# Output projection and FFN norm by quarters instead of halves, and four low-part subtractions on GpSimd

## The reference

```python
def trunk_layer(x, pos, past, mem_k, mem_v, p):
    ...                                       # three kinds of attention, x = x + mixed @ w_out
    x = x + memory_attend(x, mem_k, mem_v, p['g_mem_q'], p['w_mem_q'], p['w_mem_o'])
    y, conv_new = conv_ffn(x, conv0, p['g_ffn'], p['w_ffn_up'], p['w_ffn_conv'], p['b_ffn_conv'], p['w_ffn_down'])
    x = x + y

def memory_attend(x, mem_k, mem_v, g, w_q, w_o):
    q = (rmsnorm(x, g) @ w_q)                 # 4 heads of 128
    s = einsum(q, mem_k) * MEM_SCALE          # 256 memory tokens
    return einsum(softmax(s), mem_v) @ w_o    # 512 -> 1024

def conv_ffn(x, conv_prev, g, w_up, w_conv, b_conv, w_down):
    u = rmsnorm(x, g) @ w_up                  # 1024 -> 2 * 2816
    c = causal_conv3(u, conv_prev) + b_conv
    a, b = jnp.split(c, 2, axis=-1)
    return (jax.nn.silu(a) * b) @ w_down, ext[:, T:]
```

## Time and profile before

| | |
|---|---|
| median of 3 runs (lowest, highest) | 1674.61 us (1671.82, 1675.45) |
| the profiled execution, its own time | 1671.71 us |
| its span in the profile | 1669.9 us |
| TensorE busy (share) | 1625.0 us (97%) |
| VectorE, ScalarE, GpSimd busy | 1171.4, 675.1, 471.2 us |
| memory loop from step 8, to the end of unit 1 | 784.27 to 931.2 us of the span |

### The profile page before, as it was taken

The page is one execution under the profiler, slowest core; times in us unless marked ns, Lnnn a source line. Parts: engine busy times, 40 slices in busy tenths (PEclk is TensorE's granted clock), DMA queues, the critical chain, the costliest instruction groups (busy, mean ns, idle before and its releaser), DMA issues.

```text
span 1669.9 us, 29448 instructions
## 1 busy us (share of the span) xinstructions
PE 1625.0 (97%) x11153; PEld 1500.0 (90%) x11153; DVE 1171.4 (70%) x1602; ACT 675.1 (40%) x1283; POOL 471.2 (28%) x246
## 2 busy tenths in 40 slices
PE   9999999999999999999987999999999999999998
PEld 8999889776667799998887999999999999999987
DVE  7583577896666755437588888888888867766765
ACT  7320122586566542106344555555555542011022
POOL 2683142000000214331424333332223322433332
PEclk9999999999999999999989999999999999999999
DMA  5322110320222314316412122222222236223213
GB/s 211 99 82 83 63 62 37 111 85 16 75 90 70 115 56 152 122 38 271 173 59 69 61 79 79 79 79 78 64 65 67 79 115 230 84 78 107 88 54 114
DMA packets 71236, 155.93 MB, mean 93 GB/s; under 512 B 29680, under 2 KB 32976, under 8 KB 68336
## 3 DMA queue, kind: packets, MB, share of 16 engines
q1 hardware_dynamic: 68848, 145.33, 25.5%
q10 hardware_dynamic: 2304, 9.44, 1.7%
HBM read 119.61 MB, written 32.86 MB: 91 GB/s over the span
## 4 chain that ended last, share of the span: by engine, by line
PE 89%; DVE 5%; issue 2%; ACT 2%; POOL 1%; DMA 1%; SPq 0%; DVEq 0%; ACTq 0%; POOLq 0%
PE scores L2675 21%; PE scores L3399 20%; PE bank L2675 10%; PE bank L3399 8%; PE pair L2675 7%; PE scores L2981 3%; PE bank L3041 3%; PE pair L3065 2%; PE scores L2771 2%; PE scores L2693 1%; DVE kbuf L2203 1%; PE pair L3335 1%; PE pair L2684 1%; PE scores L3004 1%; PE pair L3099 1%
## 5 line engine op out<-in xcount | busy, mean ns | idle before, releaser
L3399 PE MATMUL scores<-c,up_w 128*128 128x288 f32 x2464 | 364.4, 297 | 10.0 <-DVE c L2431 3.2
L3399 PEld LDWEIGHTS scores<-c,up_w 128*128 128x128 f32 x2464 | 343.5, 190 | 11.8 <-issue 8.7
L1142 POOL TENSOR_TENSOR w_hi<-w_raw,zero 128x1024 fp32r<-128x1024 f32 x32 | 64.0, 2001 | 578.7 <-DVE prob L2219 262.2
L2675 PE MATMUL scores<-s_hi,w_down 128*128 128x384 f32 (+2 forms) x484 | 132.8, 334 | 0.0
L1876 ACT ACTIVATE s_hi<-s_raw 128x1152 fp32r<-128x1152 f32 x22 | 24.3, 1157 | 178.5 <-DMA s_raw<-s_mid 178.5
L2675 PEld LDWEIGHTS scores<-s_hi,w_down 128*128 128x128 f32 x484 | 88.1, 188 | 0.6
L1272 POOL TENSOR_TENSOR w_down<-down_raw,zero 128x1024 fp32r<-128x1024 f32 x20 | 37.9, 1894 | 175.4 <-PE scores L2675 80.2
L1145 POOL TENSOR_TENSOR w_lo<-w_raw,w_hi 128x1024 fp32r<-128x1024 f32 x32 | 86.6, 2707 | 2.5
L2675 PE MATMUL scores<-act_hi,w_hi 128*128 128x384 f32 x240 | 81.7, 340 | 0.9 <-POOL w_lo L1145 0.9
L2602 DVE TENSOR_TENSOR xd<-scores,xd 128x384 f32<-128x384 f32 x108 | 58.8, 553 | 33.3 <-PE scores L2675 33.3
L3399 PE MATMUL bank<-xq,up_w 128*128 128x288 f32 x528 | 79.0, 299 | 2.1 <-issue 2.1
(11 more groups left out here) (464 smaller groups left out, 4267.4 us busy)
## 6 DMA issues: line engine op xcount, KB each, us to landing
w_raw<-wstream SPq DMA_DIRECT2D x42, 512.0 KB, 3.6
s_raw<-s_mid SPq DMA_DIRECT2D x11, 1152.0 KB, 5.4
up_raw<-wstream SPq DMA_DIRECT2D x22, 512.0 KB, 4.2
x<-wstream SPq DMA_DIRECT2D x22, 512.0 KB, 4.3
s_mid<-conv SPq DMA_DIRECT2D x22, 512.0 KB, 2.8
down_raw<-wstream SPq DMA_DIRECT2D x22, 512.0 KB, 4.8
x_blk<-xT ACTq DMA_DIRECT2D x8, 576.0 KB, 4.7
x_mid<-x_blk ACTq DMA_DIRECT2D x8, 576.0 KB, 3.1
```

What stands on the lines that cost most here:

```text
L1142: pool.tensor_tensor(w_hi[:, k], w_raw[:, k], zero[:].unsqueeze(2).to_broadcast([P, KB, P]), ALU.add).then_inc(w_rounded, 1)
L2675: mm = pe.matmul(out, w[:, k, at + kb], x(kb), start=first and kb == 0 and n == 0, stop=last and kb == n_kb - 1 and n == 2)
L3399: mm = pe.matmul(bank[acc][:, 0:QF], up_w[i][:, w, tile(kb)], b[:, kb], start=i in (0, 1, 3) and kb == 0 and n == 0, stop=kb == 3 and n == ...
```

## The change

The projection goes by pairs of rows: 16 chunks of 24 matmuls, each two rows times one quarter, into a pair of banks, ordered by quarter. Six of them stand in steps 9 to 14 of the memory loop, all six in banks (1, 3); behind it the pairs (4, 5), (0, 1), (2, 3) rotate. Four weight blocks are loaded, each once; the third and fourth are split on GpSimd into tiles of their own, mo_w, once the sample scores of step 8 and of step 9 are made. Residual rows 4 to 7 are loaded before the loop, rows 0 to 3 in step 8. The norm goes by quarters of 288 columns: a square takes two rows at once, add_rows folds the two halves, and each quarter has its own sums, roots, inverse and spread on TensorE. VectorE's and ScalarE's orders of the stage are written anew. The low parts of factors 5 and 6 of each half move from VectorE to GpSimd (part_low); there those of p = 0 stand behind the last weight low part of unit 0, those of p = 1 behind two weight sums of unit 1. The loads of unit 1's weights wait for low_made too. Two weight roundings on ScalarE and two low parts on GpSimd of the reloaded blocks go.

The core of the diff: the tables, the two new parts of GpSimd's queue, and the end of VectorE's step in the memory loop (TensorE's memory_output moves by one step likewise).

```diff
-MO_ROWS = ((0, 1), (2, 3), (6, 7), (4, 5))
-MO_CHUNKS = [(m, h) for pair in MO_ROWS for m in pair for h in range(2)]
-MO_EARLY = 7
-MO_BANKS = [(1, 3)[d % 2] for d in range(MO_EARLY)] + [0] + [(2, 4, 0, 3, 1, 5)[d % 6] for d in range(N_MO - 8)]
+MO_ROWS = ((6, 7), (4, 5), (0, 1), (2, 3))
+MO_CHUNKS = [(slot, q) for q in range(4) for slot in ((0, 1, 2, 3) if q < 3 else (2, 3, 0, 1))]
+MO_EARLY = 6
+MO_BANKS = [(1, 3)] * MO_EARLY + [((0, 1), (2, 3), (4, 5))[(d + 2) % 3] for d in range(N_MO - MO_EARLY)]
+SUM_BEHIND, SPREAD_BEHIND = {6: 0, 9: 1, 13: 2}, {7: 0, 10: 1, 14: 2}
...
+            for n in range(2):
+                slot = W_MO + 2 + n
+                k = slot % 2
+                pool.wait_ge(w_loaded[k], 16 * (slot // 2) + 16)
+                pool.wait_ge(ms_ready, NTILE + 1 + n)
+                pool.tensor_tensor(mo_w[n][:, 0], w_raw[:, k], zero[:].unsqueeze(2).to_broadcast([P, KB, P]),
+                                   ALU.add).then_inc(w_rounded, 1)
+                pool.wait_ge(w_rounded, slot - 1)
+                pool.tensor_tensor(mo_w[n][:, 1], w_raw[:, k], mo_w[n][:, 0].bitcast(F32),
+                                   ALU.subtract).then_inc(w_split, 1)
...
+            def part_low(i, p):
+
+                pool.wait_ge(x_rounded, part_rounded(i, p))
+                if p:
+                    pool.wait_ge(b_made, made_no("combined", p, 3))
+                pool.tensor_tensor(act_lo_of(i, p), x_source(i, p), act_hi_of(i, p).bitcast(F32),
+                                   ALU.subtract).then_inc(low_made, 1)
+
+            part_low(5, 0)
+            part_low(6, 0)
             up_sum_3(1)
             up_sum_2(1)
+            part_low(5, 1)
+            part_low(6, 1)
...
-                if 0 <= n - NTILE < MO_EARLY:
-                    memory_residual(n - NTILE)
+                if n - NTILE >= 4:
+                    add_square(0, n - NTILE - 3)
+                if n - NTILE == 6:
+                    add_rows(0)
+                if 0 < n - NTILE <= MO_EARLY:
+                    memory_residual(n - NTILE - 1)
```

More of the change, by code:

```diff
@@ L194, in part_split, with made_no, part_made, summed_no @@
 def part_split(i, p):
[L195 to L206, removed]
+    return 2 * KB + 5 * p + PART_LO[p].index(i) + 1
+B_ORDER = [step for p in range(2) for step in
+           [("scaled", 2 * p + h, half) for h in range(2) for half in range(2)] + [("combined", p, n) for n in range(4)]]
+def made_no(*which):
+    return B_ORDER.index(which) + 1
+def part_made(i, p):
+    q = 2 * p
+    return made_no(*(("scaled", q, 0), ("scaled", q, 1), ("combined", p, 1), ("combined", p, 3), ("combined", p, 0),
+                     ("combined", p, 2), ("scaled", q + 1, 1))[i])
+def summed_no(q, j):
+    return 2 * KB + 4 * q + j
 FIRST_ORDER = [(i, p) for p in range(2) for i in range(7)]
@@ new lines, in quarter_inverse, with scale_rows @@
+            def quarter_inverse(q):
+                dve.wait_ge(sum_used, Q_FFN + q + 1)
+                dve.reciprocal(quarter_root[0:NF, q], quarter_root[0:NF, q]).then_inc(rstd_ready, 1)
+            def scale_rows(q, half):
+                dve.wait_ge(y_spread, q + 1)
+                dve.wait_ge(x_out[q % 2], 64 * (q // 2) + 64)
+                for m in range(4 * half, 4 * half + 4):
+                    last = dve.scalar_tensor_tensor(x[:, m, quarter(q)], x[:, m, quarter(q)], const("g_ffn", m),
+                                                    bank[6 + q % 2][:, 0:QF], ALU.mult, ALU.mult)
+                last.then_inc(b_made, 1)
@@ new lines, in _ @@
+            add_square(1, 3)
+            add_rows(1)
+            memory_residual(8)
+            scale_rows(0, 1)
+            split_part(0, 0)
+            memory_residual(9)
+            split_part(0, 1)
+            add_square(2, 1)
+            quarter_inverse(1)
+            memory_residual(10)
+            add_square(2, 2)
+            scale_rows(1, 0)
+            scale_rows(1, 1)
+            memory_residual(11)
+            combine(0, 0)
+            combine(0, 1)
+            memory_residual(12)
@@ new lines, in _ @@
+            add_square(2, 3)
+            add_rows(2)
+            combine(0, 2)
+            split_part(0, 4)
+            memory_residual(13)
+            split_part(0, 2)
+            add_square(3, 1)
+            combine(0, 3)
+            quarter_inverse(2)
+            memory_residual(14)
+            add_square(3, 2)
+            split_part(0, 3)
+            scale_rows(2, 0)
+            memory_residual(15)
+            scale_rows(2, 1)
+            add_square(3, 3)
+            add_rows(3)
```

351 lines of the change are left out of this document (175 added, 176 removed).

## The result

The changed kernel took 1680.47 us (median of six runs, 1678.76 to 1682.01), the kernel before 1673.21 in the six runs beside them: a ratio of 1.0039, with a 95% interval of 1.0024 to 1.0055. The change costs some 7 us. 1682.5 was forecast, in a range of 1675.5 to 1690. The profiled execution of the changed kernel has a span of 1678.8 us, that of before 1669.9, so +8.9 by the profiles; the walk of the forecast had +8.4. One execution of e1 took 6586 us and is left out of its median.

A forecast was written before the change was run, and what follows sets the result against it. It took VectorE's queue, not TensorE, as the bound around the projection and first units. Its stretches, 84.8 + 41.0 + 27.0 = 152.8 us against 144.4, gave +8.4 and so 1683.0, stated as 1682.5; range 1675.5 to 1690.

The forecast's parts named there:

- the walk of the forecast: Five engine queues followed with priced durations and VectorE/GpSimd holds, from step 8's scores to the third unit; +8.4 us.
- The loop: Memory loop, steps 8 to 14: waits for the reused bank pair and two waits in step 8; +8.9 us.
- Rival 2: No change: the loop's waits are made up behind it, where TensorE waits for VectorE anyway; +1, 1675.5 us, chance 0.09.
- The projection stage: Behind the loop: +1.4 us of work, waits 5.3 against 6.3 before; first product 84.8 us behind the mark, before 75.9.
- The first unit: First FFN unit: 41.0 us against 41.7 before, as work of 23.8 and waits of 17.2.
- (5,0): First unit: this product waits 2.0 us for its low part, late on GpSimd behind weight low part 5.
- (6,0): First unit: this product waits 4.2 us for a join on VectorE behind two scalings and two combines, the first held 2.15.
- (3,1): First unit: this product waits 6.35 us for VectorE's last low part, behind other work and holds by GpSimd.
- GpSimd's low parts: Mostly first unit: with the four low parts on VectorE again, the walk gives 3.7 us less in all.
- (1): Rival: faster, quartered norm takes its waits off TensorE if VectorE stays ahead of its list; -9, 1665.5 us, chance 0.08.
- (3): Rival: low parts on GpSimd cost nothing, the banks do; +3.8 to +4.7, 1679 us, chance 0.14.
- (4): Rival: waits in steps 12 to 14 bring the slow clock into the loop; +12 to +16, 1688 us, chance 0.13.

The follow-up runs named there:

- e1: Changed kernel with VectorE's add of each early chunk put ahead of its copy of the transposes in the memory loop; 1670.93 us.
- e8: Changed kernel with GpSimd's split of the third weight block held until the last prompt block's probabilities are normalised; 1677.9 us in one run.
- e2: Changed kernel with the four low parts of factors 5 and 6 back on VectorE; 1678.95 us.
- e3: Changed kernel with both edits, the add ahead of the copy and the four low parts on VectorE; 1668.91 us.
- e9: e7 with the four low parts of factors 5 and 6 on GpSimd again; 1662.01 us.
- e7: e3 with VectorE's order behind the memory loop written anew and GpSimd's split of the third weight block begun later; 1657.45 us.
- e5: e3 with the inverses of quarters 1 and 2 moved ahead of other work in VectorE's queue; 1667.59 us.
- e6: e3 with the four low parts of factors 5 and 6 made by no engine, high parts read instead; 1668.17 us.

## Why the prediction was right

**The loop (+8.9 forecast).** The five waits for a reused pair were put at 0.8, 0.8, 2.0, 2.35 and 1.3 us; the trace has 0.74, 0.74, 1.93, 2.07 and 1.17, for instance the third:

```profile
811.38 0.37 PE L2751 MATMUL scores<-om_hi,mo_w 128*128 128x288 f32 x1 [1.93 <-DVE x L2445]
```

The two waits of step 8 were put at 0.7 and 0.9 and came out at 0.51 and 0.64. Of the two bounds named for the second, that with GpSimd first held: its rounding started at 785.70, 0.04 us ahead of VectorE. Chunk 6 started at 827.70 (827.6 forecast). That this is so near is in part luck: TensorE was idle 7.8 us in the stretch, not 8.9, and busy some 1.0 us longer than walked. Rival 2 fell with e1.

**The projection stage (84.8 from the mark to the first product; 87.45 measured, 2.5 of it allowed for the clock).** The spreads waited 0.33, 1.57 and 2.52 (5.3 forecast in all, 4.4 measured), with a last wait of 0.21 ahead of sums 2. So the waits were 0.7 us shorter than forecast, and the stage 2.65 longer for the clock: chunk 15 and the spread ahead of it ran from 864.95 to 871.91, mostly at 1.2 GHz, and the chunk's 24 matmuls stood 0.24 us apart (0.13 at 2.4 GHz) and took 5.7 us where 3.2 were priced. The terms of this stage as written (8.9, 1.4 and 5.3 less 6.3, on 75.9) come to 85.2, where the forecast used 84.8.

**The first unit (41.0; 41.66 measured).** The sum is right and its terms are not: work 23.8 and waits 17.2 were forecast, and TensorE was busy 30.1 us and idle 11.6. Each long wait is shorter than its term: sums 3 2.50 (3.85), (5,0) 0.59 (2.0), (6,0) 3.26 (4.2), (3,1) 4.62 (6.35). The mechanism of (5,0) is wrong too: its wait is for a hold, and GpSimd's low part came in time. The join ahead of (6,0) came sooner because the combines were held 0.6 us and not 2.15, as GpSimd's two low parts had ended at 888.06. The 5.6 us lie in the busy time instead, which is 6.3 above the term, as the granted clock was 0.84 in the unit and 0.66 from 864 to 874. The walk sets TensorE at full speed and lets it wait; here it ran slowly and, as far as VectorE was the later of the two, arrived in time all the same. What the clock did cost can be followed on the marks. By the walk's terms (on 784.46) sums 3 start at 876.3, (3,1) at 902.95, and the second unit at 910.3; measured are 877.8, 903.95 and 913.6. So 1.4 us were lost at chunk 15, for which VectorE itself waited, 1.0 was left at (3,1), and 2.3 more were lost behind it, where no long wait is left to hide them (clock 0.74 from 904 to 914). The second unit gave back 0.5. That makes 2.8, where 2.5 was allowed in all (155.3 forecast with it, 155.6 measured). The allowance was taken over from the kernel before and not derived for this one, so that it fits is luck in part; e8, with the same lists behind the loop and a higher clock, takes 152.7 us for the whole, 0.7 of the difference by its later split.

**GpSimd's low parts (+3.7).** This term was too large for the changed order: 1.5 (e2 against the changed kernel) to 2.0 us (e3 against e1). In e9's order it is 4.6. What failed is that the walk with the four on VectorE kept the other waits, and they grew (the wait of (6,0), 3.26 to 4.15). The price of a hold isn't fixed; it depends on whether the held engine has the next late thing in its queue.

**Second unit (27.0).** 26.5 measured, as before. Its waits for hold and join stayed.

**The step to the median.** The forecast of 1682.5 adds the walk to a median of 1674.61 for the kernel before; six runs give 1673.21, and so a difference of 7.3 us (interval 4.0 to 9.2) where the profiles have 8.9. The profiled execution of the kernel before was one of its fastest, and the forecast took that lead for the changed kernel too, whose profiled execution (1680.61) lies at its median. That is the greater part of the 2 us by which 1682.5 was too high.

**The rivals.** (1) named a condition, that VectorE stays ahead of its list. The changed order doesn't meet it; e7's does, and that kernel stands 15.6 us below the one before. (3) was as near as the forecast on its term: 1.5 to 2.0 us lie between nothing and 3.7. (4) didn't occur in the changed kernel, whose loop has a clock of 1.00, and was seen in e2; its price of about 4 us for ten microseconds at 0.66 is too high: from 864 to 874 the 46 matmuls were busy for 9.05 us, 2.9 more than at 0.133 us each.

## What to carry to other kernels

Where the same PSUM bank or pair takes consecutive chunks, its eviction belongs ahead of anything in that queue that waits for later work of TensorE; five such waits cost 7 us here and moving two lines took them out (e1). Price an added norm or a finer staging by the position of its inverse and its sums in the evicting engine's queue, and change that whole order at once: single moves handed most of the wait on (e5, 1.3 us), the whole order, with the later split, gave 11.5 (e7). Work moved to an engine that holds the busy one is judged in the order that is otherwise best, where its price was 4.6 us and not the 1.5 seen in a poor one.

## What the runs showed of the hardware beyond the forecast

- GpSimd's rounding with a broadcast second input (`zero`) held VectorE as the subtractions do: 2.93 us for the normalising beside it, 1.23 when it stood later (e8). The Trainium skill, SBUF — State Buffer, section "SBUF: two separate sides", describes the port pair that VectorE shares with GpSimd as an exclusive lock; the trace agrees: the normalising ended at 788.67, 1.1 us behind GpSimd's end at 787.59, which is nearly its own length.
- With both queues full, neither engine goes at its own pace: GpSimd's four subtractions took 3.1 to 3.75 us each where 2.63 was seen beside a nearly free VectorE (e9), and VectorE's 2.4 to 3.4 in place of 1.35.
- A shorter list on the late engine doesn't bring the clock back by itself (e6: 0.82 in the unit, 0.87 in e3 with the longer list); an order without long waits did (e7: 1.00 in the projection, 0.95 in the unit, 0.997 over the span against 0.992).
- The cost of a slow stretch depends on what waits next: at chunk 15, for which VectorE waits, it was paid (1.4 us), and so it was behind product (3,1), the last with a long wait (9.6 us from there to the second unit, 8.8 in e8); over the whole unit three quarters of it were hidden in waits for VectorE (e8 against the changed kernel).
- Open: why the clock fell inside the loop in e2 and not in the changed kernel, whose loop is nearly the same work. One profile of each can't tell, and it wasn't tried further.
